# Order of the first loads and of the first weight slots in a two-layer hybrid decoder trunk

## The chip, the cores and the metric

The kernel runs on one core of one Trainium2 chip. The metric is the device time of one launch in microseconds (us); the number that counts is the median of several runs.

## The reference, cut to what matters

The input `x` is 512 tokens x 1024 channels, float32. There are two layers, and each does this:

```python
h = rms_norm(x, attn_pre_g[l])
u = h @ w_in[l]                        # 1024 -> 2560, ten blocks of 256 columns
y_a = conv_mixer(u[:512])              # a * sigmoid(gate), causal depthwise conv of 31 taps, LayerNorm, silu
y_b = retention(rq, rk, rv, rg)        # chunks of 128 tokens, rotary, decay, group norm, gate
y_c = moba_attention(mq, mk, mv)       # causal softmax attention in blocks of 256 tokens
y_d = pool_mixer(u_pool)               # causal means over 2/4/8/16 tokens, small matmul
x = x + rms_norm(concat(y_a, y_b, y_c, y_d) @ w_out[l], attn_post_g[l])
h = rms_norm(x, ffn_pre_g[l])
f = (silu(h @ w_gate[l]) * (h @ w_up[l])) @ w_down[l]      # hidden width 2816
x = x + rms_norm(f, ffn_post_g[l])
```

## The kernel before, in words

All weights are cut into **slots** of 128 x 2048 numbers: per layer 10 slots of `w_in` (one block of 256 columns each), 4 of `w_out`, 22 of gate and up, 11 of `w_down`. A slot comes in four **parts** of 128 x 512 float32 (256 KB). A part lands in one of four raw buffers (`raw`, `NRAW = 4`), the scalar engine (ACT) writes its high half in float16 into a ring of 8 slots (`split_hi`, line 758), the vector engine (DVE) writes the float16 rest (`split_lo`, line 1134), and each product is then three float16 matmuls (`split3`, line 493). The activations are split in the same way: `hT` holds the normalised, transposed activations, high and low.

The DMA queue is SP's. It loads x tiles 0 and 1 (128 tokens each, 512 KB), the gains of the first norm (512 KB) and the identity matrix, then the parts in order; part n waits until `lo_split` has reached n - 3, that is, until DVE has read the part that had the same raw buffer. After part 7 come x tiles 2 and 3, after part 11 the constants (1.3 MB) and eight small transfers of pool weights.

TensorE (PE) works through `UNITS`: a unit is one slot for one set of tokens. The ten `w_in` slots run in groups of four, four and two; within a group first all slots for tokens 0-255 (s=0), then all for tokens 256-511 (s=1). Slots 0 and 1 are the conv mixer's value and gate (`CONV_A`, `CONV_G`), slots 2 and 3 the attention's q and k (`MQ`, `MK`), slots 4 to 9 `MV, RQ, RK, RV, POOL, RG`. The output bank of a `w_in` unit is its number modulo 4, so a bank is taken again four units later, once its reader is done (`take`, `last_read`). A `w_in` unit has 16 **ticks** of three matmuls of 256 columns, a `w_out` unit 4 ticks of three matmuls of 512 columns, and the table `AT` says at which tick each of the mixers' small products is slipped in (`small_products`): for instance `pre_T` t, the transposes of x tile t (line 497), `moba_stage` k, the attention's scores and outputs. The mixer part of layer 0 is ticks 0 to 319, `w_out` begins at tick 320, and its units for tokens 256-511 at tick 352.

ACT and DVE have their own orders written out by hand, line after line in a loop over the layers. On DVE the work is: `norm_x` (a chain of small instructions, lines 1143 to 1157, for the reciprocal root, then the scaling, line 1207), `h_lo_of` (line 1215), `split_lo`, `glu` (line 1231), the 62 conv taps for each half of the tokens (`conv`, line 1255), the attention's maxima (`m_max`, line 1437), masks, norms and gates. On ACT: `square_x` (line 779), `split_hi`, `h_hi_of`, copies and exponentials. At the start of the program the orders are

```python
square_x("pre", 0, 0)        # ACT: x tile 0, x tile 1
square_x("pre", 0, 1)
split_hi(0)
h_hi_of("pre", 0, 0)
h_hi_of("pre", 0, 1)

norm_x("pre", 0, 0)          # DVE
norm_x("pre", 0, 1)
split_lo(0)
h_lo_of("pre", 0, 0)
h_lo_of("pre", 0, 1)
split_lo(1, 2)
```

and PE transposes both x tiles and then starts unit 0, for which it waits for all four parts of slot 0 (`lo_split`) and for `h_lo` of both tiles.

## Time and profile before

| | us |
|---|---|
| median of 3 runs (lowest to highest) | 1109.45 (1109.19 to 1110.07) |
| the profiled execution, own time | 1109.05 |
| its span, first to last instruction | 1107.2 |
| PE busy in the span | 1079.1 (97%) |
| DVE busy | 620.5 (56%) |
| ACT busy | 410.3 (37%) |
| mean granted TensorE clock | 0.999 |

The span is what the views of the profile cover; the profiled execution's own time is 1.85 us more. A row of the timeline gives the start, the time taken, the engine, the line, the operation with output<-input, the count, and in brackets how long the engine had been idle before it and what released it. PE's busy time has the pipelined matmuls in it, so a stretch in which they run at half speed also reads as busy.

### The profile page before, as it was taken

To read this page: it belongs to the slowest core of one execution; us is meant where nothing else is said; L and a number is where in the kernel's file an instruction comes from. 1 tells how busy PE (TensorE), PEld (TensorE's weight loads), DVE (VectorE), ACT (ScalarE), POOL (GpSimd) and SP (SyncE) were. 2 spreads that over 40 slices of the span, in tenths; PEclk is the share of its full clock that TensorE was granted. 3 is DMA by queue.
4 is the path that set the end of the run, shared out by engine and by line. 5 is a ranking of instruction groups with operands and counts; after the bars stand their busy time and mean duration, and the time that the engine had idled before them with its cause. 6 is when DMAs were issued, how large, how long until landed. Compare 5 with 4: busy or idle time off the path is not lost.

```text
span 1107.2 us, 16624 instructions
## 1 busy us (share of the span) xinstructions
PE 1079.1 (97%) x6640; PEld 656.5 (59%) x6640; DVE 620.5 (56%) x1418; ACT 410.3 (37%) x810; POOL 5.1 (0%) x18
## 2 busy tenths in 40 slices
PE   5999999999999999999999999999999999999997
PEld 4888785596444444444478878747844444444443
DVE  5898998884324324312568989889624324322014
ACT  4454635454323323212234463455523323322001
POOL 1000000000000000000000000000000000000000
PEclk9999999999999999999999999999999999999999
DMA  7442403155234233233003341034533333232001
GB/s 272 132 131 77 154 1 115 39 177 164 80 113 149 80 114 112 95 99 114 1 1 115 115 135 57 1 114 135 176 110 110 101 113 111 81 113 76 1 20 57
DMA packets 58172, 109.64 MB, mean 99 GB/s; under 512 B 7024, under 2 KB 7280, under 8 KB 57968
## 3 DMA queue, kind: packets, MB, share of 16 engines
q1 hardware_dynamic: 58096, 108.58, 31.1%
q8 instruction: 53, 0.87, 0.3%
q14 instruction: 23, 0.19, 0.1%
HBM read 106.46 MB, written 2.10 MB: 98 GB/s over the span
## 4 chain that ended last, share of the span: by engine, by line
PE 88%; DVE 6%; DMA 4%; issue 1%; ACT 1%; SPq 0%; ACTq 0%; DVEq 0%
PE ps L493 82%; DMA raw<-weights_dram 3%; PE ps L497 3%; DVE ring L1134 2%; DVE E L1255 2%; PE ps L696 1%; PE ps L680 1%; DMA gbc<-gains_dram 1%; DVE E L1207 0%; ACT ring L758 0%; DVE small L1437 0%; DVE hT L1215 0%; ACT gbc L758 0%; DVE U L1358 0%; PE ps L657 0%
## 5 line engine op out<-in xcount | busy, mean ns | idle before, releaser
L493 PE MATMUL ps<-hT,ring 128*128 128x512 f16 (+1 forms) x3264 | 549.0, 330 | 2.8 <-DVE hT L1215 2.7
L493 PEld LDWEIGHTS ps<-hT,ring 128*128 128x128 f16 x3264 | 320.4, 98 | 226.6 <-issue 3.1
L493 PE MATMUL ps<-ring,U 128*128 128x512 f16 x1440 | 313.4, 379 | 0.0
L1134 DVE SCALAR_TENSOR_TENSOR ring<-raw,ring 128x512 f16<-128x512 f32 x376 | 236.8, 685 | 97.5 <-ACT ring L758 96.7
L758 ACT ACTIVATE ring<-raw 128x512 f16<-128x512 f32 x376 | 212.9, 622 | 140.3 <-PE ps L493 81.2
L493 PEld LDWEIGHTS ps<-ring,U 128*128 128x128 f16 x1440 | 140.8, 98 | 167.1 <-issue 0.3
L1458 DVE SCALAR_TENSOR_TENSOR R<-ps,R 128x512 f32<-128x512 f32 (+1 forms) x52 | 31.7, 609 | 255.4 <-ACT R L933 255.0
L493 PE MATMUL ps<-ring,hT 128*128 128x256 f16 x1152 | 134.3, 273 | 0.0
L933 ACT ACTIVATE R<-ps 128x512 f32<-128x512 f32 (+1 forms) x52 | 27.5, 530 | 275.4 <-PE ps L493 275.4
L493 PEld LDWEIGHTS ps<-ring,hT 128*128 128x128 f16 x1152 | 112.2, 98 | 14.2 <-issue 1.1
L1255 DVE SCALAR_TENSOR_TENSOR E<-E,par 128x256 f32<-128x256 f32 x240 | 101.7, 477 | 0.2
L768 ACT ACTIVATE sink<-ps 128x1024 bf16<-128x1024 f32 x15 | 15.3, 1021 | 100.7 <-PE ps L493 100.7
L1143 DVE TENSOR_SCALAR small<-small 128x1 f32<-128x1 f32 x31 | 4.5, 146 | 79.6 <-ACT sink L768 71.5
L497 PE MATMUL ps<-cst,E 128*128 128x128 f32 x176 | 25.8, 287 | 10.7 <-DVE E L1207 10.1
L758 ACT ACTIVATE U<-ps 128x256 f32<-128x256 f32 (+2 forms) x48 | 21.8, 486 | 28.1 <-PE ps L497 11.7
L1465 DVE TENSOR_TENSOR U<-R,U 128x512 f16<-128x512 f32 (+1 forms) x52 | 31.1, 599 | 0.0
L497 PEld LDWEIGHTS ps<-cst,E 128*128 128x128 f32 x176 | 21.5, 148 | 13.4 <-issue 9.2
L758 ACT ACTIVATE U<-R 128x512 f16<-128x512 f32 (+1 forms) x52 | 28.9, 556 | 0.8 <-DVE R L1458 0.8
L1215 DVE SCALAR_TENSOR_TENSOR hT<-ps,hT 128x1024 f16<-128x1024 f32 x16 | 19.4, 1220 | 15.4 <-ACT hT L758 15.1
L907 ACT ACTIVATE gbc<-ps,small 128x128 f32<-128x128 f32 (+3 forms) x32 | 16.8, 525 | 19.0 <-DVE small L1437 18.5
L758 ACT ACTIVATE gbc<-ps 128x128 f32<-128x128 f32 (+3 forms) x32 | 13.9, 433 | 26.8 <-PE ps L696 21.8
L758 ACT ACTIVATE hT<-ps 128x1024 f16<-128x1024 f32 x16 | 16.3, 1021 | 19.0 <-PE ps L497 19.0
(104 smaller groups left out, 475.7 us busy)
## 6 DMA issues: line engine op xcount, KB each, us to landing
raw<-weights_dram SPq DMA_DIRECT2D x376, 256.0 KB, 3.4
gbc<-gains_dram SPq DMA_DIRECT2D x8, 512.0 KB, 6.1
xs<-x_dram SPq DMA_DIRECT2D x4, 512.0 KB, 5.3
out_dram<-xs SPq DMA_DIRECT2D x8, 256.0 KB, 2.0
cst<-consts_dram SPq DMA_DIRECT2D x1, 1296.0 KB, 8.2
bd<-pool_w_dram SPq DMA_DIRECT2D x8, 16.0 KB, 5.6
par<-params_dram SPq DMA_DIRECT2D x1, 76.0 KB, 6.0
cst<-consts_dram SPq DMA_DIRECT2D x1, 64.0 KB, 5.8
```

Source lines behind the costliest of these rows:

```text
L493: ins = mm(dst, st, mv_, start=first and i == 0, stop=last and i == 2, **kw)
L497: return nc.tensor.transpose(dst, src, ident)
L680: mm(bank[b][:, 0:P * (t + 1)], mqT[r, t % 2, h // 2, :], mkT[r, h // 2, 0:P * (t + 1)], start=False, stop=True, skip_group_check=True).th ...
L758: return A(dst, src, ACT.Copy, scale=scale)
L768: A(sink[:, :], pair(t), ACT.Square, scale=UNSCALE * DM ** -0.5, accum_out=ssq[:, t:t + 1]).then_inc(y_sq, 1)
L907: A(pr[:, h % 2, 0:w], bank[(4, 6)[h % 2]][:, 0:w], ACT.Exp, bias=nms[:, c:c + 1], accum_out=sums[:, c:c + 1]).then_inc(mP, 1)
L933: A(sil[:, n % 2, 0:P * len(tiles)], gu_tiles(f, tiles)[0], ACT.Silu, scale=UNSCALE).then_inc(sil_done, 1)
L1134: V.scalar_tensor_tensor(out=ring[:, slot % RING, 1, raw_part(part)], in0=raw[:, n % NRAW, :], scalar=W_SCALE, in1=ring[:, slot % RING, 0, ...
L1215: V.scalar_tensor_tensor(out=hT[:, 1, :, tok(t)], in0=pair(t).rearrange("p (k t) -> p k t", k=KT), scalar=A_SCALE / RN, in1=hT[:, 0, :, to ...
L1255: ins = V.scalar_tensor_tensor(out=cacc[:, c, :], in0=src, scalar=w, in1=cacc[:, c, :], op0=ALU.mult, op1=ALU.add)
L1458: V.scalar_tensor_tensor(out=fbuf[:, n % 2, 0:w], in0=gu_tiles(f, tiles)[1], scalar=UNSCALE * A_SCALE, in1=sil[:, n % 2, 0:w], op0=ALU.mul ...
L1465: V.tensor_tensor(fT[:, 1, f, span(tiles)], fbuf[:, n % 2, 0:w], fT[:, 0, f, span(tiles)], ALU.subtract).then_inc(f_lo, 1)
```

## The change

The slots are renumbered: the attention's q and k are slots 0 and 1, the conv mixer's two are slots 2 and 3. The first loads are ordered x tile 0, gains, identity, x tile 1, parts. Parts 4 to 11 (slots 1 and 2 of layer 0) don't go to the raw buffers but to the 128 x 4096 float32 that `ycat` takes up (the mixer outputs in float16, first written at the end of the attention's first half), so they wait for nothing. PE waits for slot 0 of layer 0 part by part and for `h_lo` tile by tile, DVE writes the rest of part 0, then `h_lo` of tile 0, then the other three parts. The orders of ACT and DVE and the table `AT` are written anew for both layers. The core of the diff:

```diff
+EARLY = 2 * PARTS
-CONV_A, CONV_G, MQ, MK, MV, RQ, RK, RV, POOL, RG = range(10)
+MQ, MK, CONV_A, CONV_G, MV, RQ, RK, RV, POOL, RG = range(10)
...
 AT[0]:
-        ("pre_T", 2): 55, ("pre_T", 3): 57, ("moba_T", 0): 101, ("moba_T", 1): 115, ("moba_stage", 0): 121,
+        ("pre_T", 2): 57, ("pre_T", 3): 58, ("moba_T", 0): 96, ("moba_T", 1): 107, ("moba_stage", 0): 124,
...
-        ("ret_O", 3): 304, ("conv_T", 1): 311, ("conv_Y", 1): 327, ("ret_Y", 1): 342, ("pool_Y", 1): 346,
+        ("ret_O", 3): 310, ("conv_T", 1): 315, ("conv_Y", 1): 327, ("ret_Y", 1): 343, ("pool_Y", 1): 350,
-        ... ("pre_T", 0): 948, ("pre_T", 1): 970,
+        ... ("pre_T", 0): 955, ("pre_T", 1): 965,
 AT[1]:
-        ("pre_T", 2): 35, ("pre_T", 3): 46, ...
+        ("pre_T", 2): 0, ("pre_T", 3): 31, ...
...
+        def raw_home(n):
+            if PARTS <= n < PARTS + EARLY:
+                e = n - PARTS
+                return ycat_w[:, raw_part(e)], early_in[e], 16
+            m = n if n < PARTS else n - EARLY
+            return raw[:, m % NRAW, :], raw_in[m % NRAW], 16 * (m // NRAW + 1)
...
 sync:
-            for t in range(2):
-                sp.dma_start(xs[:, t, :], x[tok(t), :]).then_inc(x_in[t], 16)
+            sp.dma_start(xs[:, 0, :], x[tok(0), :]).then_inc(x_in[0], 16)
             gain_load(1, 0)
             sp.dma_start(ident, consts[:, 0:P]).then_inc(ident_in, 16)
+            sp.dma_start(xs[:, 1, :], x[tok(1), :]).then_inc(x_in[1], 16)
...
-                if n >= NRAW:
+                if n >= PARTS + EARLY + NRAW:
                     sp.wait_ge(lo_split, n - NRAW + 1)
+                elif n >= PARTS + EARLY:
+                    sp.wait_ge(lo_split, n - EARLY - NRAW + 1)
...
 tensor, in unit():
+                by_parts = l == 0 and i == 0
-                if FIRST_OF[slot] == i:
+                if FIRST_OF[slot] == i and not by_parts:
                     pe.wait_ge(lo_split, PARTS * (l * SLOTS + slot + 1))
...
-                if pre:
+                if pre == "fpre":
                     pe.wait_ge(h_lo, xno(pre, l, tiles[-1]) + 1)
...
+                            if pre and k == 0:
+                                pe.wait_ge(h_lo, xno(pre, l, tiles[c]) + 1)
+                            if by_parts and c == 0 and k % 2 == 0:
+                                pe.wait_ge(lo_split, k // 2 + 1)
...
 scalar, start of a layer:
-                glu_tanh(l, 0)
                 ...
                 split_hi(z + 4)
                 h_hi_of("pre", l, 2)
+                moba_in(l, 0, 0)
                 h_hi_of("pre", l, 3)
-                moba_in(l, 0, 0)
+                split_hi(z + 5)
                 moba_in(l, 0, 1)
-                split_hi(z + 5)
                 split_hi(z + 6)
+                glu_tanh(l, 0)
...
 vector, start of the program:
-            split_lo(0)
+            split_lo_part(0, 0)
             h_lo_of("pre", 0, 0)
+            for part in range(1, PARTS):
+                split_lo_part(0, part)
             h_lo_of("pre", 0, 1)
             split_lo(1, 2)
 vector, start of a layer:
-                norm_y("fpost", l - 1, 3)
-                zero(l)
                 norm_x("pre", l, 2)
+                norm_y("fpost", l - 1, 3)
                 norm_x("pre", l, 3)
-                glu(l, 0)
+                split_lo(z + 4)
                 h_lo_of("pre", l, 2)
-                conv(l, 0, 1)
                 h_lo_of("pre", l, 3)
-                conv(l, 0, 4)
-                conv(l, 0, 6)
-                split_lo(z + 4)
-                moba_rotate(l, 0)
                 split_lo(z + 5)
-                conv(l, 0, 6)
+                moba_rotate(l, 0)
                 split_lo(z + 6)
+                glu(l, 0)
+                conv(l, 0, 10)
+                split_lo(z + 7)
...
 vector, end of a layer:
                 norm_y("fpost", l, 1)
-                h_lo_of("pre", l + 1, 0)
                 norm_x("pre", l + 1, 1)
-                h_lo_of("pre", l + 1, 1)
                 norm_y("fpost", l, 2)
+                h_lo_of("pre", l + 1, 0)
+                h_lo_of("pre", l + 1, 1)
```

## Rows read from the trace of the kernel before

**Rows 1.** The page, part 1: busy time of each engine.
```profile
PE 1079.1 (97%) x6640; PEld 656.5 (59%) x6640; DVE 620.5 (56%) x1418; ACT 410.3 (37%) x810; POOL 5.1 (0%) x18
```

**Rows 2.** Busy time by stretch: stretch, us, PE, PEld, DVE, ACT, POOL, clock, DMA share, GB/s.
```profile
0.00:17.00 17.00, 4.28 (x18) 3.43 (x19) 10.83 (x25) 9.01 (x13) 5.14 (x18) 1.00 0.65 217
17.00:30.00 13.00, 13.00 (x98) 10.70 (x96) 4.83 (x8) 4.16 (x7) 0.00 (x0) 1.00 0.97 338
...
43.00:200.00 157.00, 152.89 (x1224) 120.81 (x1223) 141.80 (x385) 77.48 (x174) 0.00 (x0) 1.00 0.30 95
200.00:560.00 360.00, 360.00 (x1883) 184.75 (x1882) 150.87 (x280) 117.00 (x215) 0.00 (x0) 1.00 0.33 103
560.00:720.00 160.00, 156.71 (x1348) 132.69 (x1346) 141.83 (x390) 77.48 (x169) 0.00 (x0) 1.00 0.23 74
```

**Rows 3.** Timeline of all engines, the first 43 us.
```profile
4.45 1.03 ACT L779 ACTIVATE ps<-xs 128x1024 f32<-128x1024 f32 x1 [2.44 <-DMA xs<-x_dram]
...
7.01 0.16 DVE L1157 SCALAR_TENSOR_TENSOR small<-small 128x1 f32<-128x1 f32 x1
7.80 1.28 DVE L1207 SCALAR_TENSOR_TENSOR E<-xs,small,gbc 128x1024 f32<-128x1024 f32 x1 [0.63 <-DMA gbc<-gains_dram]
8.57 2.61 ACT L758 ACTIVATE ring<-raw 128x512 f16<-128x512 f32 x4 [1.73 <-DMA raw<-weights_dram]
...
9.23 1.94 PE L497 MATMUL ps<-cst,E 128*128 128x128 f32 x8 [9.23 <-DVE E L1207]
...
11.21 1.02 ACT L758 ACTIVATE hT<-ps 128x1024 f16<-128x1024 f32 x1
11.78 2.49 DVE L1134 SCALAR_TENSOR_TENSOR ring<-raw,ring 128x512 f16<-128x512 f32 x4
...
11.91 1.97 PE L497 MATMUL ps<-cst,E 128*128 128x128 f32 x8 [0.74 <-DVE E L1207]
12.49 2.13 SPq L427 DMA_DIRECT2D raw<-weights_dram  x4
...
14.19 2.35 DVE L1215 SCALAR_TENSOR_TENSOR hT<-ps,hT 128x1024 f16<-128x1024 f32 x2
...
16.63 13.35 PE L493 MATMUL ps<-hT,ring 128*128 128x256 f16 x96 [2.75 <-DVE hT L1215]
...
20.47 5.04 SPq L438 DMA_DIRECT2D bd<-pool_w_dram  x8
...
42.68 10.65 PE L493 MATMUL ps<-hT,ring 128*128 128x256 f16 x96
```

**Rows 4.** Line 493 in the stretch 17 to 22 us: duration min/median/max.
```profile
L493 PE MATMUL ps<-hT,ring x26: 373/421/421, 16.6 to 21.9; 128*128 128x256 f16 x26
```

**Rows 5.** The same line in the stretch 24 to 29 us.
```profile
L493 PE MATMUL ps<-hT,ring x48: 272/272/273, 23.8 to 28.9; 128*128 128x256 f16 x48
```

**Rows 6.** The parts' loads, first 65 us: from issue to landing.
```profile
DMA to landing us min/median/max: 2.7/3.9/6.4
```

**Rows 7.** What PE waited for from 43 to 200 us: us in total, times, longest.
```profile
PE ps L497 <- ACT gbc L758: 1.7, 5, 0.6
PE ps L615 <- DVE R L1347: 1.1, 1, 1.1
```

**Rows 8.** The same from 560 to 720 us.
```profile
PE ps L497 <- ACT gbc L758: 2.4, 5, 1.4
```

**Rows 9.** Conv taps (line 1255) from 40 to 61.2 us: DVE busy (count), clock, DMA.
```profile
40.00:61.20 21.20, 7.20 (x18) 1.00 0.46 129
```

**Rows 10.** Low halves of weight parts (line 1134) in the same stretch.
```profile
40.00:61.20 21.20, 7.71 (x12) 1.00 0.46 129
```

**Rows 11.** Timeline of PE while the last `w_out` units run.
```profile
189.16 16.35 PE L493 MATMUL ps<-ring,U 128*128 128x512 f16 x75
```

**Rows 12.** Timeline of DVE: the last two low halves of mixer outputs; the layers' boundary.
```profile
195.13 1.28 DVE L1222 SCALAR_TENSOR_TENSOR U<-E,U 128x512 f16<-128x512 f32 x2
...
558.73 1.22 DVE L1215 SCALAR_TENSOR_TENSOR hT<-ps,hT 128x1024 f16<-128x1024 f32 x1 [10.28 <-ACT hT L758]
```

## What the change does to the time: the prediction

> **What bounds the kernel now.** I read the busy times first, then the busy time by stretch, then the timeline of the stretches in which PE isn't busy, then PE's waits in the mixers. PE is busy for 1079.1 of 1107.2 us [rows 1], so at most 28.1 us can go without taking matmuls away. The stretches say where they are [rows 2]: 12.7 us in the first 17 us (4.28 of 17 busy), 4.1 from 43 to 200 us (the mixers and `w_out` of layer 0), 3.3 from 560 to 720 us (those of layer 1), none from 200 to 560 us. Most of the rest is the program's tail, which the change leaves alone. From 200 us on a launch is one chain of matmuls, so an earlier start of PE is worth its full size unless PE waits again in a mixer stretch.
>
> A second cost is hidden in the busy time. The first 26 matmuls take 421 ns each, later ones of the same shape 272 ns [rows 4, 5], and the first 96 take 13.35 us where 96 later ones take 10.65 [rows 3]. 
>
> **How the first matmul comes to 16.63 us** [rows 3]. x tile 0 is there at 4.45; its reciprocal root is ready at 7.17; the gains, third in the queue, let the scaling begin only at 7.80. PE transposes tile 0 (9.23) and tile 1 (11.91 to 13.88). ACT splits slot 0 from 8.57 to 11.18, then makes the high half of tile 0 until 12.23. DVE does all four rests of slot 0 first (11.78 to 14.27), then the rests of both activation tiles, 14.19 to 16.54. PE waits for the last of these.
>
> **The change, part by part.**
>
> *Order of the first loads.* The gains move ahead of 0.52 MB of x, tile 1 behind them. At about 360 GB/s (my value; the stretch from 17 to 30 us has 338 [rows 2]) that is 1.45 us: the gains land near 6.3, tile 1 near 7.9 where the gains did. Tile 0's scaling then starts at 7.2, 0.6 earlier. ACT's second square ends at 7.9 + 1.03 + 0.2 = 9.1, so `split_hi(0)` runs from 9.1 to 11.7 instead of 8.57 to 11.18: 0.5 later. The root of tile 1 takes 1.55 from 9.1, the scaling 1.28: ready at 11.95, as now (11.85), so PE's second transposes stay at 12.0 to 14.0.
>
> *Slot 0 by parts, tile by tile.* DVE: scaling until 11.95, part 0 until 12.6. ACT has the high half of tile 0 at 11.7 + 1.02 = 12.75, DVE its rest at 12.8 + 1.17 = 14.0. PE can start the columns of tile 0 at 14.0, right behind the transposes, instead of at 16.63: **2.6 us**. It isn't starved: a part holds two k steps, six matmuls, 1.3 us at the lower level, and DVE makes a part in 0.62. The columns of tile 1 come after 24 matmuls, at 17.5 at the earliest; DVE has the three other parts at 15.9 and the rest of tile 1 at 17.1.
>
> *The clock.* Before, PE idled 2.75 us ahead of the first matmul; now transposes and matmuls follow each other from 12 us on. If the rise follows the same 5.4 us after unbroken work begins, it comes at 17.5 rather than 19.5, and the cost of the lower level falls from 2.7 to 1.7; if it comes at the same wall time as now (22.0), it grows to 4.0. So between +1.0 and -1.3; I take **0.5**, since the transposes are matmuls too and the gap is what differs. (The Trainium skill, page "TensorE: Matmul & The Clock Gate", section "What's actually happening", says that the window in which activity is judged runs freely and doesn't begin with the kernel, so the rise can shift from run to run. No row of one execution shows this; by that rule alone this term could be anything between the two ends, and the total shifts by it and by nothing else.)
>
> *Slots 1 and 2 without a wait.* Now DMA stands still from about 8.5 to 12.49, the first load that waits [rows 3]. With 12 parts free to go, SP issues up to the constants and the pool weights (5.04 us for those eight) and reaches part 12 near 15.6. By bytes: slot 1 is in at about 12.5, slot 2 at 18, slot 3 (8.4 MB in all) at 2 + 8.4/0.338 = 27. Slot 1 is fully split at 19.8 (DVE is free for it at 17.1), PE wants it at 20.9; slot 2 is ready at 22.5, wanted at 26; slot 3 at 28.3, wanted at 32. Slot 0 to 3 never made PE wait before, so this saves nothing of its own; it keeps the 2.6 us from being lost at slot 1, where the slack is 1.1 us.
>
> *x tiles 2 and 3.* They ready DVE earlier: norms at 31.3 and 34.1, transposes at ticks 57 and 58 (about 35), rests of h at 38.3 and 39.6. Before, the second half of the tokens began at 42.68, some 0.35 late for these. Now the first columns need only tile 2. **0.3 us.** Start of tokens 256-511: 14.0 + 2.2 + 64 ticks x 0.33 + 1.8 (transposes) = 39.2, a gain of **3.4** over 42.68.
>
> *Mixers of layer 0.* PE waits 4.1 us there. 1.7 are five waits for ACT's copies between two attention stages [rows 7]: they follow from stages put ten ticks apart, which the new table keeps. The largest single one is 1.1 us for DVE's mask of the retention scores, in a stretch in which DVE is busy for 142 of 157 us [rows 2]. Does DVE keep up with a PE that is 3.4 us ahead? Count its work to 61.2 us. Before: 18 taps and 12 parts [rows 9, 10]. After, from the order of the diff: slot 4 until 36.7, h until 39.6, slot 5 until 42, rotation 1.8, slot 6 until 46.7, `glu` 47.4, 10 taps at 0.40, slot 7, 18 taps: 61.2. That is 28 taps and 16 parts, 6.5 us more work at the same time (10 x 0.40 + 4 x 0.62). DVE is ahead by more than PE is. So the 1.1 us may go; between 0 and 1.1 I take **0.6**.
>
> *End of those mixers.* Tokens 256-511 of `w_out` need the retention output at tick 360. PE is at tick 346 at 189.3, and 42 matmuls at 0.216 later is 198.4 [rows 11]; DVE has it at 196.4 [rows 12], slack 2.0. Without an earlier DVE, 3.4 - 2.0 = 1.4 us would be given back here. The new order puts the retention ahead of the pool on both ACT and DVE, and its path starts one tick later (342 to 343), so I cost it at nothing.
>
> *Layer 1.* DVE sat idle 10.28 us before the last rest of h at the boundary [rows 12], with a finished tile to norm behind it; the new order does that first. `pre_T` 2 moves to tick 0: tile 2 is normed in time by my count (560.6 against 561.4, both in the old clock). PE's 3.3 us of waits in the mixers, 2.4 for ACT's copies [rows 8], I leave as they are: 0, with 1.5 either way. The conv chain starts about 7 us later against PE, with two slots and the rotation (6.8 us) done before it, which evens out.
>
> **Sum.** 2.6 + 0.5 + 0.3 + 0.6 = 4.0 us. The profiled execution took 1109.05, so 1105.05; the median of the runs is 0.4 above it: **1105.5 us**.
>
> **Rivals.**
>
> *Bank of the conv value taken late (slower).* With the conv slots third and fourth, the bank of `CONV_A` for tokens 0-255 is taken again at tick 96 (39.2 + 10.65 = 49.9), and `glu`, which frees it, now stands behind slots 5 and 6 on DVE and behind `split_hi` of slot 6 on ACT. Each of these parts is loaded only when a raw buffer is free and lands 2.7 to 6.4 us later [rows 6]. By the median of 3.9 `glu` ends at 47.4, 2.5 us in time. At the longest, 6.4, four turns of the buffers (slots 4 to 7) put DVE 4 x 2.5 = 10 us later. Its lead over PE (6.5 - 3.4 = 3.1) and the slack at the end of the mixers (2.0, above) take 5.1 of that, and 4.9 us are lost, half of them already at tick 96. In both layers 9.8 against 4.0 gained: 1115; half as bad, **1110.5**. It makes the kernel slower once a layer loses over 2.0, that is 7.1 us late over four turns, a turn of about 5.7 us. Against it: the loads behind are few once x and the constants are in. Chance 0.10.
>
> *The mixers give it back (no change).* DVE or ACT sets the pace at the end of the mixers after all, through the latencies between conv norm, transposes and gates, which no count of work shows. Loss 1.4 in layer 0 and 1.5 in layer 1, and the 0.6 does not come: 1109.45 - 0.5 = 1108.5 at worst, 1107.5 in the middle. For it: DVE busy 142 of 157 us [rows 2]. Chance 0.20.
>
> *The head doesn't get shorter as written.* x tile 1 lands later than 7.9 (it shares the engines with the parts behind it) and with it, on ACT, everything to the first matmul; or the clock rises at its old wall time. 1.3 to 1.5 of the gain go: 1106.9. Chance 0.10.
>
> *The new tables also remove waits.* All PE waits in both mixers halve: 3.7 instead of 0.6: 1102.4. The table was shifted where DVE was late, but nothing in the rows shows that ACT's copies get nearer. Chance 0.14.
>
> **Numbers.** The forecast has 0.46, with its own range 1104.2 to 1106.8. The range for 8 in 10 reaches from the better case, 1102.5, to 1109.0, which leaves out the slower rival and a corner of the better. About 0.2%, 2.2 us, can be told from no change. Faster (below 1107.2): nearly all of the forecast, the better case, a third of the giving back and six tenths of the shorter head: 0.71. Same: 0.19. Slower: 0.10.
>
> **What would show it.** The first matmul of line 493 at 14.0 with no idle behind the transposes; 421 ns rows for 16 to 26 matmuls; the tokens 256-511 starting at 39.2; DVE's first conv tap near 47.4; PE idle of 3 to 4 us in each mixer stretch; the gate and up stretch starting about 4 us earlier than now in layer 0. It is wrong if PE waits for `glu` (line 1231) near 50 us, if PE waits for a part of slot 1 at 21 us, or if the start of the FFN of layer 0 has gained under 2 us although the first matmul gained 2.6.

## The result, and the profile after

| | before | changed |
|---|---|---|
| median of 4 runs each, us (lowest to highest) | 1109.76 (1109.19 to 1111.80) | 1101.05 (1100.52 to 1101.62) |
| the profiled execution, own time / span, us | 1109.05 / 1107.2 | 1100.93 / 1099.1 |

The ratio is 0.9921, with a 95% interval of 0.9906 to 0.9936: 0.8% faster, 8.7 us. The forecast was 1105.5 us with a range down to 1102.5, so the sign was right and the size, 4.0 us of gain, less than half of what came.

The page of the changed kernel, part 1 (against [rows 1]): PE has as much to do as before, less 2.9 us, DVE the same, and the span is 8.1 us shorter.

```profile
PE 1076.2 (98%) x6640; PEld 656.3 (60%) x6640; DVE 620.9 (56%) x1418; ACT 409.3 (37%) x810; POOL 5.2 (0%) x18
```

Busy time by stretch of the changed kernel (columns as in [rows 2]):

```profile
0.00:17.00 17.00, 6.57 (x31) 5.24 (x32) 10.46 (x25) 9.30 (x15) 5.19 (x18) 1.00 0.91 334
17.00:30.00 13.00, 13.00 (x122) 11.65 (x120) 9.11 (x20) 8.08 (x15) 0.03 (x1) 1.00 0.82 263
30.00:43.00 13.00, 13.00 (x122) 11.84 (x120) 11.62 (x24) 7.32 (x13) 0.00 (x0) 1.00 0.51 158
43.00:200.00 157.00, 153.28 (x1207) 119.21 (x1205) 142.12 (x392) 77.33 (x175) 0.00 (x0) 1.00 0.27 84
200.00:560.00 360.00, 360.00 (x1901) 186.58 (x1900) 155.19 (x290) 116.59 (x215) 0.00 (x0) 1.00 0.32 103
560.00:720.00 160.00, 158.89 (x1346) 132.67 (x1344) 139.81 (x379) 79.00 (x173) 0.00 (x0) 1.00 0.27 85
```

The first 17 us have 6.57 us of PE work instead of 4.28, and DMA moves 334 GB/s there instead of 217. From 43 to 200 us PE is idle for 3.7 us (4.1 before), from 560 to 720 us for 1.1 us (3.3 before). The counts say more than the busy time does: between 17 and 30 us both kernels read 13.00 of 13, but the changed one gets 122 matmuls done and the old one 98.

The timeline of the changed kernel's head (against [rows 3]), DVE's, ACT's and PE's rows up to the first tokens 256-511:

```profile
7.36 1.28 DVE L1228 SCALAR_TENSOR_TENSOR E<-xs,small,gbc 128x1024 f32<-128x1024 f32 x1
8.27 1.03 ACT L796 ACTIVATE ps<-xs 128x1024 f32<-128x1024 f32 x1 [2.52 <-DMA xs<-x_dram]
...
9.33 2.28 ACT L775 ACTIVATE ring<-raw 128x512 f16<-128x512 f32 x4
...
12.23 0.68 DVE L1147 SCALAR_TENSOR_TENSOR ring<-raw,ring 128x512 f16<-128x512 f32 x1
...
12.37 1.97 PE L509 MATMUL ps<-cst,E 128*128 128x128 f32 x8 [1.64 <-DVE E L1228]
12.83 1.22 DVE L1236 SCALAR_TENSOR_TENSOR hT<-ps,hT 128x1024 f16<-128x1024 f32 x1
...
14.15 11.93 PE L505 MATMUL ps<-ring,hT 128*128 128x256 f16 x96
...
36.18 2.13 PE L505 MATMUL ps<-hT,ring 128*128 128x256 f16 x18
38.15 10.64 PE L505 MATMUL ps<-ring,hT 128*128 128x256 f16 x96
```

Where the 8.1 us of the two profiled executions are, by four points of PE's timeline:

| point | before | changed | gained so far |
|---|---|---|---|
| first matmul of slot 0 | 16.63 | 14.15 | 2.48 |
| first matmul of tokens 256-511 | 42.68 | 38.15 | 4.53 |
| first matmul of `w_out`, layer 0 | 170.58 | 165.38 | 5.20 |
| first matmul of `w_out`, layer 1 | 710.27 | 702.24 | 8.03 |

So 2.48 come from the earlier start, 1.42 from the first 96 matmuls (13.35 to 11.93), 0.63 from waits and small gaps ahead of tokens 256-511, 0.67 from the mixers of layer 0, and 2.83 from the stretch between the two `w_out`, which ends with the mixers of layer 1. Where the last are is in the stretch from layer 1's first late transposes (561.36 before, 556.17 changed) to its `w_out`; first before, then changed:

```profile
561.36:710.27 148.91, 145.62 (x1293) 127.42 (x1292) 132.60 (x346) 72.14 (x156) 0.00 (x0) 1.00 0.25 79
```

```profile
556.17:702.24 146.07, 144.96 (x1294) 127.57 (x1293) 128.09 (x334) 70.91 (x154) 0.00 (x0) 1.00 0.26 80
```

Idle time of PE falls from 3.29 to 1.11 there. More than half of that is one wait. Before, PE was free at 660.66 (659.11 + 1.55, the twelve products of an attention stage) and wanted the bank that ACT empties by its copy of the first head's transposed weights (128x384); it got it at 662.03. ACT made the high halves of two weight parts ahead of that copy, and had waited 1.25 us for their load:

```profile
662.03 0.52 PE L497 MATMUL ps<-cst,gbc 128*128 128x128 f32 x3 [1.37 <-ACT gbc L758]
```

```profile
660.20 1.31 ACT L758 ACTIVATE ring<-raw 128x512 f16<-128x512 f32 x2 [1.25 <-DMA raw<-weights_dram]
661.41 0.47 ACT L758 ACTIVATE gbc<-ps 128x384 f32<-128x384 f32 x1
```

In the changed kernel the same copy stands behind four parts that have all landed, and PE has no wait at that place (the `x3` row follows the `x12` row without a bracket):

```profile
646.58 2.54 ACT L775 ACTIVATE ring<-raw 128x512 f16<-128x512 f32 x4
649.16 0.49 ACT L775 ACTIVATE gbc<-ps 128x384 f32<-128x384 f32 x1
```

```profile
648.18 1.55 PE L713 MATMUL ps<-U,gbc 128*128 128x64 f32 x12
649.80 0.52 PE L509 MATMUL ps<-cst,gbc 128*128 128x128 f32 x3
```

That the four had landed is true of this execution, not of the new order. The kernel with the old load order (below) has the same code there, and ACT waits again, and PE behind it; ACT's rows, then PE's:

```profile
648.46 1.26 ACT L775 ACTIVATE ring<-raw 128x512 f16<-128x512 f32 x2 [1.08 <-DMA raw<-weights_dram]
649.63 0.47 ACT L775 ACTIVATE gbc<-ps 128x384 f32<-128x384 f32 x1
...
650.25 0.52 PE L509 MATMUL ps<-cst,gbc 128*128 128x128 f32 x3 [0.81 <-ACT gbc L775]
```

Over the profiled executions of the experiments, the wait at this place is 1.37, 1.32 and 0.96 us in the three with the old tables, orders and boundary, and in the ten with all the new ones nothing in five, then 0.24, 0.29, 0.65, 0.68 and 0.81. So the new ones make it shorter, by 0.95 us on the mean, and the profiled pair shows the largest difference there is.

### The profile page after: what moved, and what is told of

The parts are those of the page before. It is cut to its first block, busy times and chain, and to the rows that moved or that the text cites. A ratio compares the mean times of both kernels' runs of the same rounds, so it can differ in the third digit from the quotient of the medians.

```text
span 1099.1 us, 16624 instructions
## 1 busy us (share of the span) xinstructions
PE 1076.2 (98%) x6640; PEld 656.3 (60%) x6640; DVE 620.9 (56%) x1418; ACT 409.3 (37%) x810; POOL 5.2 (0%) x18
## 4 chain that ended last, share of the span: by engine, by line
PE 88%; DVE 1%; ACT 0%; issue 0%; ACTq 0%
PE ps L505 82%; PE ps L509 3%; PE ps L713 1%; PE ps L697 1%; PE ps L632 1%; PE ps L617 0%; PE ps L674 0%; PE ps L635 0%; PE ps L641 0%; ACT gbc L775 0%; DVE ps L1209 0%; DVE xs L1212 0%; DVE E L1276 0%; PE ps L694 0%; DVE R L1368 0%
## 5 line engine op out<-in xcount | busy, mean ns | idle before, releaser
L1147 DVE SCALAR_TENSOR_TENSOR ring<-raw,ring 128x512 f16<-128x512 f32 x368 | 231.1, 685 | 89.7 <-ACT ring L775 89.1
L775 ACT ACTIVATE ring<-raw 128x512 f16<-128x512 f32 x368 | 208.1, 622 | 127.9 <-PE ps L505 80.2
L796 ACT ACTIVATE ps<-xs 128x1024 f32<-128x1024 f32 x16 | 16.3, 1022 | 26.4 <-DVE xs L1196 21.3
```

Of the source, the lines that this page charges most:

```text
L775: return A(dst, src, ACT.Copy, scale=scale)
L796: A(pair(t), xs[:, t, :], ACT.Square, scale=DM ** -0.5, accum_out=ssq[:, 4 + t:5 + t]).then_inc(x_sq, 1)
L1147: V.scalar_tensor_tensor(out=ring[:, slot % RING, 1, raw_part(part)], in0=raw_home(n)[0], scalar=W_SCALE, in1=ring[:, slot % RING, 0, raw_ ...
```

## The experiments

The second median in each is that of the kernel before, timed together with it; points of the timeline are of one profiled execution each. Where a kernel is compared with the changed one, that is against its median of 1101.05, which came again at 1101.06. Each of the first four starts from the changed kernel; they ask which part of the change carries what.

**Slot 0 awaited whole.**

```diff
+                if by_parts:
+                    pe.wait_ge(lo_split, PARTS)
+                    pe.wait_ge(h_lo, xno("pre", 0, 1) + 1)
-            split_lo_part(0, 0)
+            split_lo(0)
...
```

> The changed kernel, with the first unit waiting for all four parts of slot 0 and for h_lo of both tiles, and DVE's order of before there; all else as changed. Theory (the clock follows unbroken work): DVE finishes the rest of tile 1 near 17.1, so the first matmul starts at 17.1 instead of 14.15 (3.0 later) and, with some 2.7 us of idle ahead of it, runs at the lower level for 5.4 us from there instead of 3.8: the first 96 matmuls take 13.3 us instead of 11.9. Tokens 256-511 start at 42.5 instead of 38.15, and the time is 1105.0 (4.0 more; some of it may be absorbed by the 1.0 us wait for DVE near 110 us). Rival (the rise comes on a grid of its own, not with the work): 96 matmuls in anything from 12 to 14.5 us. Rival (the mixers give it back): the start is 3 to 4.4 us later but w_out of layer 0 is less than 2 us later.

1103.55 (1103.24 to 1105.30) against 1110.41. First matmul at 16.12, tokens 256-511 at 40.50. The wait by parts and tiles is worth 2.5 us at the end of the program, 2.0 of it at the first matmul: the predicted mechanism. Expected were 17.1 and 1105.0. The first matmul is earlier than that because x tile 1 was there at 7.30, against 8.27 in the changed kernel; with the same landing it would have come near 17.1, by an estimate from these two.

**No early parts.** Slots 1 and 2 go to the four raw buffers again.

```diff
-            if PARTS <= n < PARTS + EARLY:
-                ...
-            m = n if n < PARTS else n - EARLY
+            m = n
...
```

> The changed kernel without the early parts: slots 1 and 2 go through the four raw buffers and wait for lo_split as before. My prediction gave the early parts no gain of their own. Counter-theory: without them part 4 is issued at 12.9 instead of 5.6, slot 1 is ready at about 20.8 (wanted at 20.7), slot 2 at 27 (wanted at 25.9), slot 3, behind the constants, at 34.5 (wanted at 31.3): PE waits about 3 us in all before tokens 256-511, which start at 41.2 instead of 38.15; time 1104. By the prediction's own account it would be within 0.5 us of the changed kernel, 1101.5.

1107.99 (1106.90 to 1110.25, 10 runs) against 1110.41. This is the surprise: 6.9 us slower than the changed kernel, though PE starts earlier. Timeline of PE in this kernel:

```profile
13.37 12.75 PE L500 MATMUL ps<-ring,hT 128*128 128x256 f16 x96
27.45 5.41 PE L500 MATMUL ps<-hT,ring 128*128 128x256 f16 x48 [1.33 <-DVE ring L1142]
35.49 3.12 PE L500 MATMUL ps<-hT,ring 128*128 128x256 f16 x27 [2.62 <-DVE ring L1142]
...
41.17 1.09 PE L504 MATMUL ps<-cst,E 128*128 128x128 f32 x8 [1.35 <-DVE E L1223]
...
44.81 10.64 PE L500 MATMUL ps<-ring,hT 128*128 128x256 f16 x96 [0.58 <-DVE hT L1231]
```

Slot 2 is 1.33 us late, slot 3 2.62, then x tile 3 (its load stands behind those parts in the queue) 1.35 and 0.58: 5.9 us of waits, all behind slot 1, where the prediction had looked for the danger. The counter-theory had the places right, and its 3 us of waits were half of what came.

**Old boundary.** The transposes of the next layer's x (ticks 948, 970, 35, 46) and ACT's and DVE's orders at the end of a layer as before; the orders at the start of layer 1 stay new.

```diff
-("pre_T", 0): 955, ("pre_T", 1): 965,
+("pre_T", 0): 948, ("pre_T", 1): 970,
-("pre_T", 2): 0, ("pre_T", 3): 31,
+("pre_T", 2): 35, ("pre_T", 3): 46,
...
```

> The changed kernel with the layer boundary of before: DVE and ACT make h of tile 0 before they norm tile 1, norm_y of tile 2 last, and the transposes of x tiles at ticks 948, 970, and in layer 1 at 35 and 46. Theory A (layer 1's 2.8 us come from the boundary, where DVE no longer idles 10 us): the stretch from the start of layer 1 to its w_out grows by 1.5 to 2.8 us, PE's waits there go from 1.1 back towards 3.3, time 1103.3. Theory B (they come from the order and ticks within the mixers): the stretch stays within 0.5 us, time 1101.3.

1104.59 (1104.36 to 1105.24) against 1110.41: 3.5 slower than changed. PE's waits from 560 to 720 us in this kernel:

```profile
PE ps L509 <- ACT U L775: 1.8, 1, 1.8
PE ps L509 <- ACT gbc L775: 1.4, 5, 0.4
PE ps L509 <- DVE U L1328: 1.0, 1, 1.0
```

The first and the last line are new: the attention's first transposes, which the new table has 25 and 31 ticks earlier, now come before their input. Theory A expected 1103.3: the loss is larger than the gain of layer 1 itself, so this is in part a mismatch of table and boundary, not the boundary's share.

**Warmed up.** 28 matmuls of a constant tile ahead of and between the transposes of x, so that PE is at its upper level when slot 0 begins (work added).

```diff
+            pe.wait_ge(dve_tick, 3)
+            busy(17)
+            h_T("pre", 0, 0)
+            busy(11)
+            h_T("pre", 0, 1)
...
```

> The changed kernel with 17 idle matmuls of ones (128x512 float16) on PE from 2 us on, and 11 more between the two transposes; they go to a bank that nothing reads before it is overwritten. Theory: PE is at 2.4 GHz when the first real matmul starts at 14.1; the first 96 take 10.65 us instead of 11.9 (all at 272 ns), each eight transposes 1.05 instead of 1.95, and the time falls by 1.3, to 1099.7. Rival: the level doesn't carry over the 1 us gaps behind the transposes, or the wait for slot 1 takes its place (it is split at 21.8, wanted at 14.15 + 5.3 = 19.5): then PE waits 2.3 us at slot 1 and nothing is gained, 1101 to 1102.

1100.80 (1100.56 to 1102.32) against 1110.41. The first 96 matmuls take 10.93 us instead of 11.93, each of them 269 to 283 ns, but x tile 1 landed later in this execution (8.70) and tokens 256-511 start at 37.95, with a new wait of 0.20. The level costs 1.0 us there, and the median is 0.25 lower, which does not stand clear of the spread; 1099.7 was expected.

The next two ask about layer 1 from both sides.

**Before with the new boundary** (the same lines, other way round, and the orders of the boundary).

```diff
-("pre_T", 2): 35, ("pre_T", 3): 46,
+("pre_T", 2): 0, ("pre_T", 3): 31,
...
-                norm_y("fpost", l - 1, 3)
-                zero(l)
                 norm_x("pre", l, 2)
+                norm_y("fpost", l - 1, 3)
...
```

> The kernel before with the changed kernel's layer boundary alone: norm of tile 1 and norm_y of tile 2 ahead of h of tiles 0 and 1, norm of tile 2 ahead of norm_y of tile 3, transposes at 955, 965 and, in layer 1, 0 and 31; zero and glu_tanh moved behind the norms so that nothing waits for itself. Theory (layer 1 gains because DVE starts it with less to do): the stretch from the start of layer 1 to its w_out falls from 148.9 by 1.5 to 2.5 us, its 1.4 us wait behind a late weight part goes, time 1107.5. Rival (boundary and mixer order only pay together, the gain is in the mixer order and ticks): 148.9 within 0.5, time 1109.5 to 1110.

1110.30 (1108.29 to 1111.80, 10 runs) against 1109.56: nothing, ratio 1.0004 (0.9995 to 1.0014). From `w_out` to `w_out` it is 541.0 us, 1.3 more than before: the wait behind the late weight part is 0.73 here, but a new one of 1.50 us for ACT's copy of `U` has come. The theory (1107.5) is refuted; the rival, no gain, is what came.

**Changed with layer 0's ticks in layer 1.**

```diff
+AT[1] = {**AT[0], **{k: v for k, v in AT[1].items() if k[0] in ("pre_T", "fpre_T")}}
```

> The changed kernel with layer 0's table of ticks for layer 1's mixers too (the transposes of x and of the FFN input keep theirs). Theory (DVE is 2 to 3 us further ahead in layer 1 after the new boundary, so its products could be put 10 to 30 ticks earlier, but need not be): the stretch of layer 1 stays within 0.7 us of 146.1, time 1101 to 1101.7. Rival (the earlier ticks are what removes the waits): the stretch is 147.5 to 149, PE's waits in it over 2.5 us, time 1103.5.

1103.38 (1102.96 to 1106.38) against 1109.56: 2.3 slower than changed. Waits for `U` of 0.51 (ACT) and 0.97 us (DVE) appear in layer 1, as the rival has it. The profiled execution is the slowest of the four (the others take 1102.96 to 1103.78) and shows something else as well, told at the end.

The next two undo or push on the order at the very start.

**Old load order** (x tiles 0 and 1, gains, identity), from the changed kernel.

```diff
-            sp.dma_start(xs[:, 0, :], x[tok(0), :]).then_inc(x_in[0], 16)
+            for t in range(2):
+                sp.dma_start(xs[:, t, :], x[tok(t), :]).then_inc(x_in[t], 16)
...
```

> The changed kernel with the first loads in the order of before: x tiles 0 and 1, gains, identity. By the prediction's count the scaling of tile 0 is 0.5 later (7.8) but ACT splits slot 0 from 8.5 instead of 9.3, and DVE scales tile 1 at 10.6 instead of 11.0: the first matmul comes at 13.6 to 13.9 instead of 14.15. So the theory is that the new order of the loads gives nothing or costs 0.3 us: time 1100.7 to 1101.1. Rival (the gains are what the first matmul hangs on): 0.5 later, 1101.6.

1100.20 (1099.22 to 1101.38) against 1109.56, with the first matmul at 13.16. Undoing this part of the change costs nothing.

**Tile 0 ahead of everything.** PE runs six matmuls of slot 0 before it transposes tile 1; ACT makes the high half of tile 0 behind the first part, and DVE its rest before it scales tile 1.

```diff
+                if (l, at) == (0, 2): h_T("pre", 0, 1)
-            for t in (0, 1):
-                h_T("pre", 0, t)
+            h_T("pre", 0, 0)
...
```

> A version meant to be faster than both: the changed kernel with tile 0 taken further ahead. ACT makes the high half of tile 0 after the first part of slot 0 instead of after the fourth, DVE makes its rest before it scales tile 1, and PE transposes tile 1 at tick 2 of the first unit. Theory: the first matmul starts at 13.0 instead of 14.15, the columns of tile 1 are not late, tokens 256-511 start at 37.3 instead of 38.15, time 1100.0. Rival (the rest of tile 1 comes at 18.5, and slots 1 to 3 or h of tiles 2 and 3 set the end of the head): PE waits the same amount later, time 1101.

1101.03 (1100.99 to 1101.72) against 1109.56. The first matmul moves to 13.20, but behind it stand the transposes, and the other 90 go on at 16.14. Nothing is gained; 1100.0 was expected.

Then the change was taken apart into head and rest.

**New head, old rest**: the kernel before with new load order, early parts, and slot 0 by parts; the conv value is still slot 0.

```diff
-            split_lo(0)
+            split_lo_part(0, 0)
             h_lo_of("pre", 0, 0)
+            for part in range(1, PARTS):
+                split_lo_part(0, part)
...
```

> The kernel before with the head alone changed: new order of the first loads, slots 1 and 2 loaded early into the mixer outputs' room, slot 0 awaited by parts and h tile by tile; slot numbers, tables, both orders and the boundary as before. Theory A (layer 1's 2.8 us belong to the new numbering, tables and orders): tokens 256-511 begin at 38.5 to 40, w_out of layer 1 follows its start as in the kernel before (149 us stretch), time 1105.0 to 1106.5. Theory B (the earlier PE in layer 0 is what removes the waits later on too): layer 1 in 146 to 147.5, time 1102 to 1103. Theory C (the old orders can't keep up with an earlier head, DVE late at the end of layer 0's mixers): 1.4 us or more of new waits ahead of tick 352, time above 1107.

1108.13 (1106.34 to 1112.24, 10 runs) against 1110.56; ratio 0.9978 (0.9961 to 0.9995). Theory A's 1105.0 to 1106.5 did not come. Layer 1 keeps its old length, as it has it, but tokens 256-511 begin at 41.27 and not at 38.5 to 40, and that, not the new waits of theory C, is where the time is. PE in this kernel:

```profile
16.20 12.76 PE L504 MATMUL ps<-hT,ring 128*128 128x256 f16 x96 [2.37 <-DVE hT L1233]
```

The conv slot's products take 256 tokens at once, so the first needs both tiles of `h`, and waiting by parts is empty. A q slot takes the 128 tokens of one tile at a time. So the start at 14.15 needs both the renumbering (without it 16.20) and the finer wait (without it 16.12).

**Early parts alone**, in the kernel before.

```diff
-                sp.dma_start(raw[:, n % NRAW, :], weights[n, :, :]).then_inc(
-                    raw_in[n % NRAW], 16)
+                dst, landed, _ = raw_home(n)
+                sp.dma_start(dst, weights[n, :, :]).then_inc(landed, 16)
...
```

> The kernel before with nothing changed but where slots 1 and 2 of layer 0 land (the mixer outputs' room, no wait for a raw buffer). By the prediction's account (the parts save nothing of their own) 1109.0 to 1109.8. By what the kernel without them showed (reloads of slots 2 and 3 are marginal in the old head too, with up to 2.8 us of waits in one execution of it and 0.35 in another): tokens 256-511 begin at 42.3 to 42.7 in every execution, median 1108.5 to 1109.2, and the spread of the runs is under 1 us.

1107.31 (1105.88 to 1118.39, 10 runs) against 1110.56. The medians are 3.2 us apart, the interval of the ratio, 0.9960 to 1.0009, does not exclude no gain at all. Tokens 256-511 start at 40.44, with no wait behind the first matmul. A spread under 1 us was expected and came as 12.5; the slowest run has a mean granted clock of 0.990.

**Old head, new rest**: the changed kernel with old loads, no early parts, and slot 0 awaited whole.

```diff
-            m = n if n < PARTS else n - EARLY
+            m = n
-            sp.dma_start(xs[:, 0, :], x[tok(0), :]).then_inc(x_in[0], 16)
+            for t in range(2):
+                sp.dma_start(xs[:, t, :], x[tok(t), :]).then_inc(x_in[t], 16)
+                if by_parts:
+                    pe.wait_ge(lo_split, PARTS)
+                    pe.wait_ge(h_lo, xno("pre", 0, 1) + 1)
...
```

> The changed kernel with its head put back: old order of loads, no early parts, slot 0 awaited whole. New numbering, tables, orders and boundary stay. If the rest of the change stands on its own, the layer 1 stretch (561 to 710 us before) is 146 to 146.5 and the time is that of the kernel before less 2.8 to 3.5: 1106 to 1107, with a first matmul near 16.5. If the new orders need the early parts (they put slots 2 and 3 ahead of more work), tokens 256-511 start later than 43.5 and 1108 to 1109.5 comes out.

1106.82 (1105.16 to 1109.46, 10 runs) against 1110.56; ratio 0.9970 (0.9956 to 0.9984). Busy time of this kernel in layer 1's mixers:

```profile
560.00:720.00 160.00, 158.67 (x1359) 134.15 (x1358) 137.78 (x377) 77.88 (x171) 0.00 (x0) 1.00 0.25 76
```

1.3 us idle (1.1 in the changed kernel), though PE comes to `w_out` of layer 0 4.7 us later. The head of it starts tokens 256-511 at 42.87, after waits of 1.33 and 0.58.

**Old load order and a shorter warm-up** (17 and 7 matmuls), a candidate for less than 1100.

```diff
+            busy(17)
+            h_T("pre", 0, 0)
+            busy(7)
+            h_T("pre", 0, 1)
...
```

> The changed kernel with the old order of the first loads and 24 matmuls of a constant tile ahead of and between the transposes of x (17 and 7), so that the clock has risen before the first real matmul. If the price of the lower level is all that is left there (1.0 to 1.3 us over the first 96 matmuls) and the loads are as good in the old order: 96 matmuls in 10.7 to 10.9, tokens 256-511 at 37.0 to 37.5, 1099.3 to 1100.2. If what is gained is waited for again at the parts of slots 1 to 3 or at h of tile 3, 1100.3 to 1101.

1101.38 (1101.25 to 1102.53) against 1110.56. First matmul 13.79, 96 in 10.93, and then 0.33 and 0.58 of waits for x tile 3: what was gained is waited for again. It is no faster than the changed kernel.

**Changed again, and with the old load order again**, timed together on one chip. The first has no edit; the second has that of the old load order.

> The changed kernel as it is, timed again beside the next one on the same chip. If its time is as steady as the four runs so far (1100.5 to 1101.6), the median is 1101.0 and the spread under 1.5 us; the first 96 matmuls take 10.9 to 12.4 us, whatever this execution's clock does.

> The changed kernel with the old order of the first loads (x tiles 0 and 1, then gains and identity), timed again beside the changed one. If the new load order is worth what the prediction gave it (tile 0 scaled 0.6 us earlier, so the first matmul 0.6 earlier), this is 0.6 us slower, 1101.6. If it is worth nothing, 1101.0. If the earlier single measurement was real (first matmul 13.16 instead of 14.15), this is 0.8 us faster, 1100.2.

1101.06 (1100.34 to 1101.60, 6 runs) and 1100.61 (1099.56 to 1101.56, 6 runs), before 1109.97. The old load order is 0.45 us faster here and 0.85 in the first pair, neither of which stands clear of the spread. Its profile says why it isn't slower; timeline of ACT, DVE and PE in the second:

```profile
5.70 1.03 ACT L796 ACTIVATE ps<-xs 128x1024 f32<-128x1024 f32 x1
...
7.67 1.29 DVE L1228 SCALAR_TENSOR_TENSOR E<-xs,small,gbc 128x1024 f32<-128x1024 f32 x1 [0.52 <-DMA gbc<-gains_dram]
...
8.40 2.69 ACT L775 ACTIVATE ring<-raw 128x512 f16<-128x512 f32 x4 [1.56 <-DMA raw<-weights_dram]
...
13.56 11.44 PE L505 MATMUL ps<-ring,hT 128*128 128x256 f16 x96
```

Tile 0 is scaled 0.3 us later than in the changed kernel, but ACT squares tile 1 at 5.70 instead of 8.27, and the first matmul comes 0.6 earlier. Which of the two orders is ahead hangs on one landing each, as the executions with a start by tiles show together (us; "scaled" is the start of DVE's scaling of tile 0, "squared" that of ACT's square of tile 1, which in the new order is when the tile has landed):

| | started at | first matmul | later by |
|---|---|---|---|
| new load order, squared, six executions | 7.49, 8.16, 8.27, 8.38, 8.58, 8.70 | 13.37, 14.05, 14.15, 14.26, 14.46, 14.59 | 5.88 or 5.89 in each |
| old load order, scaled, three executions | 7.26, 7.67, 7.90 | 13.16, 13.56, 13.79 | 5.89 or 5.90 in each |

Between the two lies DVE's own order: root and scaling of tile 1, rest of part 0, rest of `h` of tile 0. In the old load order it starts from the scaling of tile 0, which waits for the gains in two of the three; in the new one it starts from the landing of tile 1.

PE's points side by side, from the profiled execution of each (us):

```
                            first    first 96   tokens    w_out     w_out 0 to
                            matmul   matmuls    256-511   layer 0   w_out 1
before                      16.63    13.35      42.68     170.58    539.69
changed                     14.15    11.93      38.15     165.38    536.86
changed again               14.05    11.93      38.04     165.63    536.87
slot 0 awaited whole        16.12    12.31      40.50     167.06    537.48
no early parts              13.37    12.75      44.81     172.81    537.45
old boundary                14.46    12.36      38.88     165.39    540.40
warmed up                   14.59    10.93      37.95     164.58    537.31
old load order              13.16    11.65      37.82     165.08    537.61
old load order again        13.56    11.44      37.07     163.95    536.85
before + new boundary       16.01    12.54      44.26     172.09    540.98
new head, old rest          16.20    12.76      41.27     169.37    539.12
early parts alone           16.02    12.10      40.44     167.78    539.40
old head, new rest          16.03    12.48      42.87     170.07    537.08
old loads, short warm-up    13.79    10.93      38.08     165.71    536.95
tile 0 ahead of all         13.20    6 + 90     39.03     165.62    537.04
layer 0's ticks in layer 1  14.26    11.67      38.00     164.90    542.78
```

The last column splits the kernels into groups. Every one with the new tables, orders and boundary together is at 536.9 to 537.6 us, whatever its head; those with the old rest at 539.1 to 539.7; and those with a boundary or ticks that do not fit the rest at 540.4 and more (the 542.78 has a fall of the clock in it, told at the end). Between the first two groups lie 1.5 to 2.8 us, and the profiled pair has the longest of the one and nearly the shortest of the other. Nearly all of the spread within a group is the wait behind the weight part: without it, the first group is at 536.8 to 537.3 and the second at 538.1 to 538.3, so that 1.3 us is steady and the rest is how late that part lands.

## Why the prediction was wrong in size

*First matmul.* Predicted 14.0, 2.6 earlier; measured 14.15, 2.48 earlier. DVE's rest of `h` of tile 0 was put at 12.8 and ran at 12.83. The mechanism was right and shown by undoing it (16.12). That only the renumbered slot allows it was left out of the working, and the new head without the new numbers shows it (16.20).

*Load order.* The gains did come in time (scaling at 7.36 without a wait), but tile 1 landed 0.4 later than put down, and the order as a whole gave nothing: with the old one the first matmul is 0.5 to 1.0 us earlier. The step that failed is to count the gains' earlier landing and to take tile 1 as ready "as now". DVE scales tile 1 before it makes the rest of `h` of tile 0, so the new order hangs the first matmul on the landing of tile 1, 5.88 us ahead of it, and the old one on the scaling of tile 0. ACT's later split is not on this path: in the changed kernel the high half of tile 0 is done at 12.52 and DVE takes it at 12.83, straight behind part 0 (12.23); with the old order again it is done at 12.09 and taken at 12.24, straight behind part 0 (11.64).

*Clock.* Put at 0.5, with bounds of -1.3 and +1.0; the profiled pair shows 1.42. The mis-sized term hides a wrong mechanism: I let the rise follow the start of unbroken work. Ninety-six matmuls at the upper level take 10.65. The excess over this, by execution, is 2.70 before, 1.28 twice with the change, and 0.79 to 2.11 in the other kernels of the table that have no warm-up. The five kernels with the same 2.75 us of idle PE ahead of the first matmul have 2.70, 1.89, 1.83, 1.66 and 1.45. So one profiled execution's 2.70 was the highest of the lot, and comparing with it overstates the gain. The rule in the Trainium skill, page "TensorE: Matmul & The Clock Gate", section "What's actually happening", that the window runs freely and does not start with the kernel, agrees with this scatter better than the rule I used. It is not shown by one kernel run twice: both executions of the changed one took 11.93.

*Early parts.* That this "saves nothing of its own" and guards only the slack at slot 1 is a step that failed. They are worth 6.9 us under the new head. The danger was looked for at slot 1 alone, for one delay; the loads of slots 2 and 3 and x tile 3 wait for the same four buffers in turn, and each inherits the lateness of the one before. The sentence "slot 0 to 3 never made PE wait before" rested on one execution. The head of the kernel before with the new boundary is the same code up to slot 3 (behind it the norms of x tiles 2 and 3 can only come sooner), and there PE waited 1.00 us for slot 3, 0.74 and 1.03 for x tiles 2 and 3, and tokens 256-511 began at 44.26 instead of 42.68. The old head was at its limit, and an execution of the kernel before can start its second half 1.6 us later than the profiled one did. For the forecast, though, this step cost little: the start of tokens 256-511 was predicted at 39.2 and came at 38.15, and the clock has most of that.

*Mixers of layer 0.* Predicted 0.6, measured 0.67. By its place it was partly luck: the 1.1 us for DVE's mask of the retention scores [rows 7] is gone, and a wait of 1.0 for DVE's `U` (line 1379) has come in the attention:

```profile
PE ps L509 <- ACT gbc L775: 2.0, 6, 0.7
PE ps L694 <- DVE U L1379: 1.0, 1, 1.0
PE ps L694 <- ACT U L775: 0.3, 1, 0.3
PE ps L509 <- ACT U L775: 0.3, 1, 0.3
```

Nor can 0.67 be told from the scatter: from tokens 256-511 to `w_out` it is 127.3 to 128.1 us in the four kernels of the table with the old tables there, and 126.5 to 128.0 in the others. The count of DVE's work up to 61 us held: first tap at 47.53, predicted 47.4, and 28 taps by 61.2.

*Layer 1 at nothing.* This is the step that failed by most: 2.83 us in the profiled pair, 1.5 to 2.8 over the kernels of the table. The prediction read the waits for ACT's copies [rows 8] as the latency of stages that stand ten ticks apart, "which the new table keeps". Neither half holds as it stands. Four of the five waits, 1.0 us together, are of that kind and came back. The fifth and longest was a copy queued behind a split whose load was late (1.37 us, above). And the table does not keep the distances: in layer 1, stages 8 to 11 moved from ticks 234, 245, 256 and 268 to 218, 254, 278 and 282. What is left of the waits is

```profile
PE ps L509 <- ACT gbc L775: 1.0, 4, 0.4
```

The parts of this gain do not add: the new boundary in the old kernel gains nothing, without it the changed kernel loses 3.5 us, layer 0's ticks in layer 1 lose 2.3. Table, boundary and orders fit each other or they don't, and no run prices one of them alone. What is steady in it, 1.3 us over the table, has in it two waits that stand in all four profiles with the old table and in none of the ten with all the new ones: 0.52 us for DVE's conv taps and 0.31 for ACT (line 907). The shorter wait behind the weight part adds 0.95 on the mean of the executions, and this pair happened to show 1.37. The old head with the new rest shows that the gain does not hang on the head. The prediction's rival with all the waits halved, at a chance of 0.14, described layer 1 (idle 3.3 to 1.1) but not layer 0 (4.1 to 3.7).

*The rival "the mixers give it back".* Its worst case is worked out wrong in the prediction: 1109.45 - 0.5 is 1108.95, not 1108.5. The forecast does not use it, and nothing was given back.

*Sum.* Of the 4.1 us that were missing in the profiled pair, layer 1 is 2.8, the clock 0.9, the waits ahead of tokens 256-511 0.3, the mixers 0.1, the first matmul -0.1. The two halves tried apart give 1108.13 and 1106.82 against 1110.56; their 2.4 and 3.7 add to 6.2, the whole gives 8.9 where it was timed again. The missing 2.7 is about the start by tile (2.5, by slot 0 awaited whole), which neither half has; that these two are the same is argued, not shown.

*Open.* ACT's and DVE's orders within the mixers were never undone by themselves, so their share beside the table's stays open, and with it why the wait behind the weight part is shorter with the new ones. 0.66 us of layer 1's gain is in PE's busy time, not its waits (145.62 to 144.96 for the same matmuls); no experiment takes it apart. Whether the new load order costs 0.4 us or nothing is inside the spread.

## What to carry to other kernels

When a stall is removed at the front of a chain of loads that share a few buffers, follow the whole chain and not the next link: each later load starts from the delayed or advanced one, and the slack of one execution is not a bound. A wait "for engine X" needs one more look, at what X was doing: the costliest one here was a copy behind a weight part that had not landed, and its length changed from one execution to the next with the same code (0 to 0.81 us). A load order is judged by the landing that the first product really hangs on, here x tile 1 or the gains, with 5.9 us of DVE's work behind it. And a finer wait helps only if the first product's operands are as fine: look at what one instruction reads before counting on it.

## What the runs showed of the hardware

The first 96 matmuls take 0.8 to 2.7 us more than the 10.65 that they take later, by execution, at granted clocks that the profile gives as 1.00 in all of them. That scatter is wider than the term of the clock in the prediction, 0.5. With 28 matmuls on a constant tile ahead, all 96 take 269 to 283 ns and 0.28 is left, so that much is not the level.

A load has no fixed landing time either. With the same loads ahead of it in the queue, x tile 1 was in use at 7.30 to 8.70 us in nine executions with the new load order, tile 0 at 4.34 to 4.65.

The clock can fall in the middle too. In the kernel with layer 0's ticks in layer 1, after 0.51 and 0.97 us of waits amid small float32 matmuls, the granted clock fell, to 0.63 in the microsecond from 651 and to 0.50 in each of the six from 652 to 658; stretches of that kernel:

```profile
640.00:650.00 10.00, 8.33 (x72) 6.65 (x69) 8.35 (x19) 8.19 (x19) 0.00 (x0) 1.00 0.56 173
650.00:660.00 10.00, 9.87 (x56) 7.68 (x57) 7.21 (x15) 6.71 (x14) 0.00 (x0) 0.66 0.41 144
```

```profile
651.38 2.82 PE L714 MATMUL ps<-U,gbc 128*128 128x64 f32 x12
...
654.63 2.77 PE L506 MATMUL ps<-ring,hT 128*128 128x256 f16 x12
```

The same 12 small matmuls take 1.55 us in the changed kernel, and 12 wide ones 1.48 a little later in this one: of the two levels, 1.2 and 2.4 GHz, this is the lower. These two rows and the eight matmuls behind them (1.06 us, 0.72 in the changed kernel) cost 2.9 us more than at the upper one. Another run of the kernel, at a mean clock of 0.999, took 1102.96 where this one, at 0.996, took 1106.38. The changed kernel had none of its ten runs under 0.998; the one before has some at 0.994 to 0.996, with 1111.6 to 1115.9 us. A few removed waits in such a stretch may thus be worth more than their length; that is argued from one trace and not shown.

With no buffer to wait for up to part 11, the queue of the changed kernel moved 327 to 442 GB/s in slices of 0.75 us from 3 to 20 us, mostly above the 360 of the prediction.
